# Wider moving operands, shifted scalings and a reordered stick loop in a three-layer transformer kernel

## The reference

```python
q = rmsnorm(q.reshape(bsz, seq, N_Q_HEADS, HEAD_DIM), q_norm_g)      # sliding-window layer, per head
p = jnp.exp(s - m)
denom = jnp.sum(p, axis=-1, keepdims=True) + jnp.exp(sink - m)
p = (p / denom).astype(v.dtype)                                      # the scaling
...
z = jnp.einsum('bhqd,bhsd->bhqs', qc, k).astype(jnp.float32) * scale # stick-breaking
log_fail = jnp.where(past, jax.nn.log_sigmoid(-z), 0.0)              # the log terms
later = lax.cumsum(log_fail, axis=3, reverse=True) - log_fail
w = jnp.where(past, jnp.exp(jax.nn.log_sigmoid(z) + later), 0.0)
...
swiglu = (jax.nn.silu(x @ w_gate) * (x @ w_up)) @ w_down
```

## Time and profile before

| | |
|---|---|
| median of 3 runs | 807.57 us (807.32 to 807.67) |
| the profiled execution | 807.54 us |
| its span | 805.7 us |
| TensorE busy | 792.5 us, 98% |
| VectorE, ScalarE, GpSimd busy | 572.4, 487.8, 88.4 us |

### The profile page before, as it was taken

How to read it: one execution, slowest core, us unless ns; L and a number is a source line. 1 busy time by engine, 2 the same in 40 slices (tenths; PEclk the granted TensorE clock), 3 DMA queues, 4 the chain that set the end, 5 groups by cost and what they waited for, 6 DMA issues and landing times.

```text
span 805.7 us, 15014 instructions
## 1 busy us (share of the span) xinstructions
PE 792.5 (98%) x5557; PEld 727.7 (90%) x5557; DVE 572.4 (71%) x860; ACT 487.8 (61%) x763; POOL 88.4 (11%) x152
## 2 busy tenths in 40 slices
PE   8999999999999999999999999999999999999997
PEld 7999999998898888889998899998999888888885
DVE  5987897977867877776458655556587787887443
ACT  7779956878665655554346555655756565555334
POOL 9405100057300000000000012000000000000000
PEclk9999999999999999999999999999999999999999
DMA  8624566543445766656665545344545576666651
GB/s 263 209 92 125 167 204 187 183 132 106 158 130 162 231 185 183 205 183 186 183 181 180 177 135 158 108 131 156 177 141 180 174 219 192 180 194 180 194 182 53
DMA packets 101045, 136.31 MB, mean 169 GB/s; under 512 B 5064, under 2 KB 86400, under 8 KB 100992
## 3 DMA queue, kind: packets, MB, share of 16 engines
q1 hardware_dynamic: 99232, 133.23, 54.2%
q0 software_dynamic: 1600, 2.28, 1.1%
q10 hardware_dynamic: 160, 0.07, 0.0%
HBM read 134.51 MB, written 1.05 MB: 168 GB/s over the span
## 4 chain that ended last, share of the span: by engine, by line
PE 89%; DVE 5%; ACT 3%; issue 1%; DMA 1%; POOL 1%; SPq 0%; ACTq 0%; DVEq 0%
PE bank L535 40%; PE bank L604 17%; PE bank L601 10%; PE bank L543 8%; PE bank L648 7%; PE bank L599 2%; DVE w_lo L1573 2%; ACT w_hi L1078 1%; ACT arena L1078 1%; PE bank L834 1%; PE bank L854 1%; DMA stage<-a_w_in 1%; PE bank L847 1%; PE bank L1041 1%; POOL arena L500 1%
## 5 line engine op out<-in xcount | busy, mean ns | idle before, releaser
L1573 DVE TENSOR_TENSOR w_lo<-stage,w_hi 128x1024 fp32r<-128x1024 f32 x249 | 303.2, 1223 | 156.6 <-ACT w_hi L1078 155.8
L535 PE MATMUL bank<-acts,w_hi 128*128 128x256 f32 (+1 forms) x1936 | 352.7, 285 | 1.8 <-DVE arena L1748 0.6
L1078 ACT ACTIVATE w_hi<-stage 128x1024 fp32r<-128x1024 f32 (+1 forms) x251 | 261.9, 1049 | 102.4 <-PE bank L535 55.0
L535 PEld LDWEIGHTS bank<-acts,w_hi 128*128 128x128 f32 x1936 | 301.4, 192 | 5.4 <-issue 3.1
L535 PE MATMUL bank<-acts,w_lo 128*128 128x256 f32 (+1 forms) x968 | 273.9, 283 | 0.0
L604 PE MATMUL bank<-acts,w_hi 128*128 128x512 f32 x616 | 217.5, 396 | 0.0
L601 PE MATMUL bank<-acts,w_lo 128*128 128x256 f32 x704 | 189.8, 280 | 0.0
L535 PEld LDWEIGHTS bank<-acts,w_lo 128*128 128x128 f32 x968 | 185.6, 192 | 0.0
L604 PEld LDWEIGHTS bank<-acts,w_hi 128*128 128x128 f32 x616 | 115.7, 188 | 25.4
L601 PEld LDWEIGHTS bank<-acts,w_lo 128*128 128x128 f32 x704 | 132.7, 188 | 3.6
L1078 ACT ACTIVATE arena<-bank 128x512 f32<-128x512 f32 (+1 forms) x79 | 43.6, 561 | 70.4 <-PE bank L604 46.8
(11 more groups left out here) (188 smaller groups left out, 670.9 us busy)
## 6 DMA issues: line engine op xcount, KB each, us to landing
stage<-ffn_w_gate SPq DMA_DIRECT2D x44, 512.0 KB, 4.1
stage<-ffn_w_up SPq DMA_DIRECT2D x44, 512.0 KB, 4.5
stage<-ffn_w_down SPq DMA_DIRECT2D x44, 512.0 KB, 3.6
stage<-w_in SPq DMA_DIRECT2D x40, 512.0 KB, 3.7
stage<-a_w_in SPq DMA_DIRECT2D x24, 512.0 KB, 4.5
stage<-b_w_in SPq DMA_DIRECT2D x16, 512.0 KB, 3.7
stage<-a_w_out SPq DMA_DIRECT2D x12, 512.0 KB, 3.6
stage<-b_w_out SPq DMA_DIRECT2D x8, 512.0 KB, 3.5
```

The lines of the kernel that those rows point to most:

```text
L535: mm = pe.matmul(dst, w[:, slot, c:c + P], a[:, k, :] if isinstance(k, int) else a[:, bass.ds(k, 1), :], start=start and n == 0, stop=stop ...
L1078: return nc.scalar.activation(out_, in_, func, **kw)
L1573: dve.tensor_tensor(w_lo[:, n % RING, 0:w], src, w_hi[:, n % RING, 0:w].bitcast(F32), ALU.subtract)\
```

## The change

1. The sliding queries (chunks 1 to 4 of the layer) are computed by `token_piece` in banks 5 and 0, then 2 and 3, with 512 weight columns moving; `tok_out`, `head_sum` and `head_root` follow the new order, and head turn 3 stands between halves 10 and 11, with its root, sum and product behind the first scores. `swa_out(5)` moves ahead of `scored(4)`.
2. The stick values (chunks 10 and 11) are computed by `token_piece` in banks 4 and 5, and copied together in slot 23.
3. The scalings of sliding heads 14 and 15 are VectorE's (`normalise_last`) instead of GpSimd's.
4. In both FFNs the first half of pair 1's next weights, its `low_part(0)` and its `both_parts(0)` stand ahead of the wait for pair 0's SiLU.
5. In the stick rounds VectorE forms the log term of head r in round r, and splits it into a rounded part and a rest (`stick_two`); the cumulative sums are four fp32r matmuls with rounded constants that GpSimd copies, instead of two float32 matmuls.

```diff
-HEAD_ROOT = {5: (0, 1), 6: (2,), 8: (3,)}
-HEAD_TURN = {6: (0, 1), 8: (2,), 9: (3,), 11: (4,)}
+HEAD_ROOT = {5: (0,), 6: (1,), 7: (2,)}
+HEAD_TURN = {6: (0,), 7: (1,), 8: (2,), 11: (4,)}
+SWA_TWO = ((5, 0), (2, 3))
...
+        def stick_two(n):
+
+            two_parts = acts[:, 16 + 2 * (n % 2):18 + 2 * (n % 2), :, :].rearrange("p k s t -> p (k s t)")
+            return two_parts[:, 0:SC], two_parts[:, SC:2 * SC]
+
+        tri, all_ones = acts[:, 24, 0, 0:P], acts[:, 24, 0, P:T]
         def stick_ln(n):
...
             stream(C_KV, 1, lambda j: col(I["w_kv"], j))
-            stream(C_Q, 8, lambda j: col(I["b_w_in"][0], j))
+            col_pairs(C_Q, 2, I["b_w_in"][0])
+            stream(C_Q + 4, 4, lambda j: col(I["b_w_in"][0], j + 4))
...
-            stream(C_MIX + 6, 14, lambda j: col(I["w_in_2"][0], j + 6))
+            stream(C_MIX + 6, 4, lambda j: col(I["w_in_2"][0], j + 6))
+            for b in range(2):
+                load(C_MIX + 10 + b, I["w_in_2"][0].rearrange("(k p) n -> p k n", p=P)[:, 4 * b:4 * b + 4, 10 * T:12 * T],
+                     split(C_MIX + 8 + b))
+            stream(C_MIX + 12, 8, lambda j: col(I["w_in_2"][0], j + 12))
...
-                if r >= 2:
+                if 2 <= r < NQ:
                     normalise(r - 2)
...
             for h in range(NH):
                 normalise(NQ + h)
+                if h == 0:
+                    pool.wait_ge(xl_ready, KD * 5)
+                    pool.tensor_copy(tri, con[:, TRI:TRI + P]).then_inc(tri_in, 1)
+                    pool.tensor_copy(all_ones, ones[:, :]).then_inc(tri_in, 1)
...
                 pe.wait_ge(hn_tok, n + 1)
                 if n >= 2:
-                    pe.wait_ge(hn_done, n - 1)
+                    pe.wait_ge(hn_done, n - 1 if n == 2 else n)
...
             def swa_half(j):
                 s, h = divmod(j, 2)
-                if h == 0 and s >= 3:
-                    last = {3: 1, 4: 0}.get(s, s - 1)
-                    if last < 5:
-                        pe.wait_ge(tok_raw, last + 1)
-                    else:
-                        pe.wait_ge(q_raw, last - 4)
-                    if last == 0:
-                        pe.wait_ge(v_raw, 2)
+                if 1 <= s < 5:
+                    if j == 6:
+                        pe.wait_ge(rb_sb, 1)
+                    token_piece(C_Q, j - 2, SWA_TWO[(j - 2) // 4], normed=2 if j < 6 else None)
+                    return
+                if h == 0 and s == 5:
+                    pe.wait_ge(tok_raw, 1)
+                    pe.wait_ge(v_raw, 2)
+                if h == 0 and s > 5:
+                    pe.wait_ge(q_raw, s - 5)
                 if s == 0:
                     col_half(C_KV, h, 4, first_tile=8, normed=1, token=True)
                 else:
-                    col_half(C_KV + s, h, swa_bank(s), normed=2 if s == 1 else None, token=s < 5)
+                    col_half(C_KV + s, h, 4)
             pe.wait_ge(con_in, 16)
...
             def turn(n):
-                pe.wait_ge(p_norm, 2 * n + 2)
+                if n < NQ - 2:
+                    pe.wait_ge(p_norm, 2 * n + 2)
+                elif n < NQ:
+                    pe.wait_ge(p_last, 2 * (n - NQ + 2) + 2)
+                else:
+                    pe.wait_ge(p_norm, 2 * n - 2)
                 if n >= 2:
                     pe.wait_ge(t_out, n - 1)
                 p = score_buf(n)
...
                     if g != 1:
                         swa_half(10 + 2 * g)
+                    if g == 0:
+                        head_turn(3)
                     swa_half(11 + 2 * g)
                 if g == 0:
                     head_turn(4)
...
                         pe.wait_ge(m_raw, 2)
                     token_piece(C_MIX, j, MIX_TWO[j // 4], normed=4 if j < 4 else None)
+                    return
+                if c in (10, 11):
+                    if j == 20:
+                        pe.wait_ge(m_raw, 8)
+                    token_piece(C_MIX + 10, j - 20, MIX_TWO[2])
                     return
                 if h == 0 and c == 6:
                     pe.wait_ge(m_raw, 4)
...
                     n = r - 2
-                    pe.wait_ge(sp_done, n + 1)
+                    if n == 0:
+                        pe.wait_ge(tri_in, 2)
+                    pe.wait_ge(sp_hi, n + 1)
                     if n >= 2:
                         pe.wait_ge(d_done, n - 1)
-                    sums, sp_n = bank[2 + n % 2], stick_sp(n)
-                    pe.matmul(sums[:, 0:SC], con[:, TRI:TRI + P], sp_n, start=True, stop=False, skip_group_check=True)
-                    pe.matmul(sums[:, P:T], ones[:, :], sp_n[:, T:SC], start=False, stop=True, skip_group_check=True)\
+                    sums, (sp_h, sp_l) = bank[2 + n % 2], stick_two(n)
+                    pe.matmul(sums[:, 0:SC], tri, sp_h, start=True, stop=False, skip_group_check=True)
+                    pe.matmul(sums[:, P:T], all_ones, sp_h[:, T:SC], start=False, stop=False, skip_group_check=True)
+                    pe.wait_ge(sp_lo, n + 1)
+                    pe.matmul(sums[:, 0:SC], tri, sp_l, start=False, stop=False, skip_group_check=True)
+                    pe.matmul(sums[:, P:T], all_ones, sp_l[:, T:SC], start=False, stop=True, skip_group_check=True)\
                         .then_inc(c_done, 1)
                 if r >= 5 and r % 2 == 0:
                     h = r - 6
...
             def tok_out(n):
-                act.wait_ge(ring_free, half_of(C_KV) + 2 + 2 * n)
+                act.wait_ge(ring_free, half_of(C_KV) + (2, 6, 6, 10, 10)[n])
                 if n >= 3:
                     act.wait_ge(hn_turn, n - 1)
                 w = P if n == 0 else T
                 for tb in range(TB):
-                    y = f(by_tok(n)[:, tb * w:(tb + 1) * w], bank[swa_bank(n)][:, tb * T:tb * T + w], ACT.Identity,
+                    src = bank[SWA_TWO[(n - 1) // 2][tb]][:, (n - 1) % 2 * T:(n - 1) % 2 * T + T] if n else \
+                        bank[4][:, tb * T:tb * T + w]
+                    y = f(by_tok(n)[:, tb * w:(tb + 1) * w], src, ACT.Identity,
                           scale=n_rstd[:, tb:tb + 1])
                 y.then_inc(tok_raw, 1)
                 act.wait_ge(tok_raw, n + 1)
...
                     tok_out(0)
-                    tok_out(1)
                 for n in HEAD_ROOT.get(j, ()):
                     head_root(n)
-                if j in (5, 7):
-                    tok_out(j // 2)
+                if j == 5:
+                    tok_out(1)
+                    tok_out(2)
                 if j != 9:
                     for n in HEAD_TURN.get(j, ()):
                         head_out(n)
                 hi(48 + j)
             for j in range(9):
                 swa_slot(j)
+            tok_out(3)
             tok_out(4)
-            head_out(3)
+            head_root(3)
             head_root(4)
             act.preload_act_table(ACT.Exp)
...
             softmax_exp(0, 1)
             softmax_exp(1, 1)
+            head_out(3)
             swa_slot(9)
             softmax_exp(2, 1)
...
                 def pair(j, i=0):
-                    def low_part(u):
+                    def low_part(u, j=j):
                         act.wait_ge(ring_free, base + 4 * j - 2 + 2 * u + i * 8)
                         f(tiles((40, 36)[u] + 2 * (j % 2), 2).rearrange("p (t n) -> p t n", t=2),
                           two[ffn_two(n, j, u)][:, :, T:2 * T], ACT.Copy).then_inc(ff_low, 1)
-                    hi(base + 4 * j, i, 8)
-                    low_part(0)
+                    if j != 1:
+                        hi(base + 4 * j, i, 8)
+                        low_part(0)
                     hi(base + 4 * j + 1, i, 8)
                     if j == 0:
                         hi(base + 2)
                         hi(base + 3)
                         root(2 * n + 2)
                         act.preload_act_table(ACT.Silu)
+                        hi(base + 4)
+                        low_part(0, 1)
                     act.wait_ge(ff_g, first + j + 1 + i * 2)
                     gate = tiles(40 + 2 * (j % 2), 2)
                     f(gate, gate, ACT.Silu).then_inc(ff_silu, 1)
...
                 act.wait_ge(ring_free, half_of(C_MIX) + 2 * c + 2)
-                if c == 5:
-                    for tb in range(TB):
-                        v = f(tiles(16 + 2 * tb, 2), bank[MIX_TWO[2][tb]][:, :], ACT.Identity, scale=n_rstd[:, tb:tb + 1])
-                    v.then_inc(m_val, 2)
-                    return
                 for tb in range(TB):
-                    at = 20 * T + tb * 512 + (c % 2) * T
-                    v = f(flat[:, at:at + T], bank[4 + c % 2][:, tb * T:(tb + 1) * T], ACT.Identity,
+                    v = f(tiles((16 if c == 5 else 20) + 2 * tb, 2), bank[MIX_TWO[2][tb]][:, :], ACT.Identity,
                           scale=n_rstd[:, tb:tb + 1])
-                v.then_inc(m_val, 1)
+                v.then_inc(m_val, 2)
             def branch_hi(b):
...
```

(63 more changed lines are left out.)

10 lines of the change are left out of this document (5 added, 5 removed).

## The result

The changed kernel takes 810.96 us (median of 6 runs, 810.83 to 812.35), the kernel before 807.47 us beside it: ratio 1.0046, 95% interval 1.0036 to 1.0057. That is 3.5 us slower; 810.9 was forecast. The profiled execution has a span of 808.9 us for 805.7, 3.2 us more; the terms summed to 3.3.

What follows compares the result with a forecast made beforehand. TensorE, busy 98% of the span, was taken to set the end outside a few stretches. Terms summed to +3.3 us, led by +4.4 at piece 20; 805.7 + 3.3 + 1.84 gave 810.9 us, range 806.3 to 813.0.

Steps and rivals of the forecast that it cites:

- The largest term: Stick values: piece 20 waits for bank 5, freed by VectorE's late scaling of mix chunk 9; +4.4 us.
- ring not late: Rival: chunk 9's scaling is done by 489.8, so piece 20's wait and clock loss go; 805.2 us, chance 0.12.
- The clock: About 4.2 us idle at piece 20 drops TensorE's clock to half for 2.6 us; +1.3 us (bounds 0 and 2.6).
- Scalings 14 and 15, and the FFN pairs: VectorE's scalings remove the wait before turn 15, -1.56 us; earlier additions start both FFNs' third pairs sooner, -1.38 us.
- Turn 3: Head turn 3 behind the first scores waits 1.3 us for VectorE; half 12 starts +0.4 us later (bounds -0.6, +1.4).
- X: Start of the first sliding score matmul, put at 168.3 instead of 169.5; times around turn 3 count from it.
- item 1: Sliding queries: 512-column matmuls replace 256-column ones, 12.5 ns saved a pair, leaving 0.9 us saved.
- savings reach the end: Rival: no wait at turn 3, stick rounds set by TensorE, clock held; some 807 us, chance 0.10.
- Item 7: Stick values: copying chunks 10 and 11 together makes ScalarE's table load and first log term 0.6 us later.
- item 5: Stick values in 512 columns: 48 pairs save 0.55 us, but piece 20 waits for bank 5, +4.4 us.
- Item 8: Stick rounds: cheaper sums save TensorE 2.3 us, but VectorE's added work eats it; stage ends 0.1 us later.
- stick sums released by the subtraction: Sign of being right: in the stick rounds TensorE's sums wait for VectorE's subtraction, which frees their bank.

Runs made afterwards that it cites:

- e2: Changed kernel with VectorE's scaling of mix chunk 9 moved one slot earlier, to slot 18 ahead of that slot's rest: 805.73 us.
- e3: Changed kernel with 18 extra 512-column matmuls, results overwritten, in TensorE's wait at piece 20: 809.22 us.
- e1: Kernel before with only the stick values in 512-column pieces (their transfers, wait for chunk 9's addend, one copy of both): 814.9 us.
- e11: Changed kernel with the scaling of mix chunk 9 one place later, behind the rest of its slot: 812.68 us.
- e4: Kernel before with only two parts: the earlier FFN pair 1 addition and scalings 14 and 15 on VectorE: 804.55 us.
- e6: Kernel of e2 with head turns 3 and 4 moved later on TensorE, turn 3 in bank 0, and q_raw(1) one place earlier on VectorE: 805.78 us.
- e10: Kernel of e9 with all of the sliding queries' part as before (256 columns, turn 3 ahead of the scores): 803.26 us.
- e5: Kernel of e2 with the stick rounds' log terms and cumulative sums as before the change: 806.27 us.
- e9: Kernel of e2 with one ScalarE table load less, and VectorE's scalings of the stick rounds' filling chunks ahead of its wait for the logarithm: 803.98 us.
- e7: Changed kernel with 8 extra 512-column matmuls in TensorE's wait at piece 20: profiled execution 809.47 us, the other four 810.82 to 811.03.

## Why the prediction was right, and where its steps were not

The time was right to 0.1 us, and mostly for the reasons given. Some of the agreement is luck: by the table the clock with the cheaper pieces was 0.3 us dearer than forecast, the stick rounds 0.5 cheaper, the scalings gave 0.1 less; and around turn 3 two misses of about 0.3 us cancelled, as told below.

**The largest term** was right in place, cause and size: 4.41 us for 4.4, released by the scaling of chunk 9. e2 shows the cause: the same scaling one slot earlier takes 5.2 us off. It also shows that what the forecast said against "ring not late", that VectorE's idle time is ScalarE's work, is true and beside the point: the ring need not be faster, since the scaling never needed to stand behind it.

**The clock** fell, and e3 shows what it cost, apart from the wait. 1.3 was forecast; the profiled execution paid 1.4, and by the medians of e3 it was 1.7 to 2.0, so this term was mis-sized, inside its bounds. That the low level lasts as long as it took to fall was a guess without a row, and the runs do not show it: 3.9 us to the fall and 3.4 low in the changed kernel, 3.4 and 6.8 in e1, 2.9 and 6.8 in e11. In those two the first matmul came 0.8 and 2.5 us behind the fall, in the changed kernel 0.3; three cases don't make it a rule. It may also be why the changed kernel's six runs reach up to 812.35: the two longest (811.64 and 812.35) have the lowest mean clock, 0.995 for 0.996 to 0.997. It isn't shown, as the clock in stretches is on record only for the one at 810.83. The Trainium skill, page "TensorE: Matmul & The Clock Gate", section "HAM oscillation", has half rate after an idle gap between bursts. The traces agree for the waits of 4.17, 4.18 and 5.47 us; after the 0.58 us of e2 and the 1.28 at turn 3 the clock stayed at 1.00.

**Scalings 14 and 15, and the FFN pairs**: -1.46 and -0.69, -0.68 for -1.56 and twice -0.69, and e4 shows that they reach the end.

**Turn 3** starts 5.92 us behind the first scores (5.9 forecast), the table load 4.52 (4.4), q_raw(1) is ready at 11.75 (11.8); half 12 at 180.62 (180.55). What failed is the first number of it, X: 168.65 instead of 168.3. TensorE waits at head turn 1 for VectorE's product, which stands behind a rest: the turn starts 0.50 us behind the start of the last matmul of its half (161.61), where the next one usually follows in 0.23. That wait was not in my sum, a pair gave less than I took (9 ns, see the last section), and the 0.9 us of item 1 were really some 0.5. Half 12 came out right all the same, because TensorE's own way from turn 3 to it took 6.05 us (174.57 to 180.62) where my times leave 6.35 (174.2 to 180.55). That is luck.

```profile
159.99 1.23 DVE w_lo L1610
...
161.37 0.70 DVE arena L1906
...
162.11 0.66 PE bank L810 x4
```

The rival "savings reach the end" priced the wait at turn 3 at 1.3 us. e6 shows that it is worth nothing, because the wait moves; and e10 shows that the whole part costs 0.7 us.

**Sums and copy.** Item 7 was 0.6 and measured 0.78 (e1). In item 5 the 48 pairs at 12.5 ns make 0.6 us, not 0.55; at the 9 ns measured they gave 0.4. Item 8 was mis-sized, beyond its lower bound of -0.25: +0.1 forecast, -0.59 measured (62.20 us for the rounds in the changed kernel, 62.79 in e1), -0.54 in e5. TensorE's own part was near: a head's four matmuls take 0.63 us for 0.58 (start to start 0.28, 0.06, 0.23, 0.06), against 0.78 to 0.89 before:

```profile
520.30 0.44 PE L1074 MATMUL bank<-acts 128*128 128x384 f32 x1
520.58 0.22 PE L1075 MATMUL bank<-acts 128*128 128x128 f32 x1
520.64 0.39 PE L1077 MATMUL bank<-acts 128*128 128x384 f32 x1
520.87 0.22 PE L1078 MATMUL bank<-acts 128*128 128x128 f32 x1
520.93 0.45 PE L553 MATMUL bank<-acts,w_hi 128*128 128x256 f32 x2
```

VectorE's copy was dearer than I took (0.40 us to the next instruction, 0.35 forecast), its term too (0.59 for 0.47), the difference as taken (0.48 for 0.5), and still the stage was shorter: my round by round layout was too slow by some 0.7 us, and it put TensorE's wait at the subtraction. The trace has it at the scalings of the filling chunks, and e9 shows that VectorE's order alone makes those. By the mark that I set, "stick sums released by the subtraction", this step was wrong, though over 1.1 us of waits were there (2.9 as the profile counts them).

## What to carry to other kernels

A matmul that is made wider to save 9 ns of 240 a pair also writes more banks at once, and waits for the last of them; before such an edit, look at who frees each bank and at what stands ahead of it in that engine's order. Here one scaling that could have been issued 3.6 us earlier (488.32 in e2, 491.87 in the changed kernel) turned a gain of 2.0 us into a loss of 3.5. When an engine waits in a fixed order, put what is ready already ahead of its waits (e2 and e9, 5.2 and 1.7 us for moves of a line). And a saving on TensorE is worth nothing in a stretch that a chain of the other engines sets (e6), even where the profile shows a wait that could be taken away.

## What the runs showed of the hardware

- The clock fell 3.9, 3.4 and 2.9 us after TensorE's last matmul had ended (changed kernel, e1, e11), 2.6 at the kernel's end. It held through 1.3 us (turn 3), 0.6 us (e2) and, in the profiled execution of e7, 2.4 us.
- It came back 3.2 us after TensorE's first matmul behind the wait in the changed kernel, 6.0 in e1, 4.3 in e11. A wait of the same length (4.17 and 4.18 us) so cost 1.4 or 2.7 us on top of itself, and the longer one of e11 1.9; what sets how long the low level lasts is open.
- A matmul of rounded values in 128 columns is followed by the next in 0.06 us, though that one has other weights (L1075 to L1077): half of the 0.115 that I took, and at my lower bound of 0.066.
- A pair of 256 columns turned into one of 512 gave 9 ns: the pieces 21 to 23 with what lies between them take 11.37 us (496.83 to 508.20) for 11.69 (492.83 to 504.52), 0.32 us for 36 pairs. By the earlier trace rows I had 12.5. The rule of the Trainium skill that the prediction set against them (page "TensorE: Matmul & The Clock Gate", section "Back-to-back issue gap") gives an estimate of 2.5, and the trace lies nearer the rows.
